# Query latents' squares behind their copy, a later first turn group, and an up projection in runs of one width

## The chip, the cores and the metric

The kernel runs on one core of one Trainium2 chip. The metric is the device time of one execution in microseconds; the time before is the median of three runs. The core has TensorE (matmuls, writing to PSUM), VectorE, ScalarE, GpSimd and SyncE, which work side by side, each through its own queue in order, and wait for each other by semaphores. The profile calls them PE, DVE, ACT, POOL and SP.

## The reference

A decoder trunk of two layers on 256 tokens of width 2048, in float32. Layer 0 mixes with stick-breaking and forgetting attention, layer 1 with latent attention; behind each mixer stands an MLP with squared ReLU. What the change touches is the latent attention and the MLPs' first matrix:

```python
def mla_mixer(h, positions, w_down, q_a_g, kv_a_g, w_uq, w_ukv, q_g, k_g, w_o):
    down = h @ w_down                                    # 2048 -> 512 + 512 + 64
    c_q, c_kv, k_pe = jnp.split(down, [512, 1024], axis=-1)
    c_q, c_kv = rmsnorm(c_q, q_a_g), rmsnorm(c_kv, kv_a_g)
    q = to_heads(c_q @ w_uq, 16)                         # 16 heads of 128 + 64
    kv = to_heads(c_kv @ w_ukv, 16)                      # 16 heads of 128 keys + 128 values
    ...
    q, k = rmsnorm(q, q_g), rmsnorm(k, k_g)              # then rotary positions on the 64
    return causal_softmax_attention(q, k, v) @ w_o

def squared_relu_mlp(h, w_up, w_down):                   # 2048 -> 8192 -> 2048
    return jnp.square(jax.nn.relu(h @ w_up)) @ w_down
```

## The kernel before

**Products in two halves.** Every float32 operand is split into a rounded half (hi) and a residual (lo), and a product is hi·hi + hi·lo + lo·hi. Weights arrive by DMA in loads of four k-tiles; half a load is a *piece*. For each piece ScalarE writes hi (`split_hi`, L766) and VectorE lo (`split_lo`, L1075), four pieces ahead of TensorE (`AHEAD`); the next hi into a buffer waits until TensorE has used the old piece (`pieces_used`).

**The order of the work.** `plan_steps` writes out by hand, for each piece `n` of a mixer, the steps that follow it. TensorE, ScalarE and VectorE walk the same list: TensorE runs the piece and then its part of the steps; the other two run their parts of the same steps in the list's order, the split of piece `n + 4` among them (normally first). An engine that waits in a step holds everything behind it in its queue.

**Layer 1's mixer.** Its chunks come in the order ckva, ckvb (key latents, 512, and the shared rotary key), cq (query latents), then ukv0, uq0, ukv1, uq1 up to uq7: for each *group* g of two heads the keys and values (`ukv{g}`, 512 wide, two pieces of twelve matmuls) and the queries (`uq{g}`, 384 wide, two pieces). Around them stand these steps:
- `rows` of a chunk: ScalarE copies the sums out of PSUM (L833); for ukv and uq it first squares them with a sum (`square_rows`, L838). Two pairs of banks serve in turn, so a chunk may not start before the rows of the chunk two before it are read (`rows_read`).
- `latent_scale(which)`: the root of a latent's mean square. ScalarE squares the latents in SBUF (`nat`), VectorE takes the mean (L1082), ScalarE a logarithm and an exponential (`power`, L774 and L775), VectorE corrects them; uq0's rows wait for the result (`scale_ready`).
- `turn_c(n)`: transposes of latents, two tiles of TensorE, a scaled copy by ScalarE (L933), a residual by VectorE (L1273). ukv0 needs 0 and 1, uq0 needs 2 and 3 (`c_ready`).
- `turn(t)`, t = 16 + 3g + 0, 1, 2: transposes of a group's scaled keys, scaled queries and rotary parts (L1670) into the one bank TURN, which VectorE then copies out (L1263, L1258, L1261). A turn waits until the turn before it is copied out (`turn_read`). The keys and queries are scaled by VectorE behind the rows of uq (L1228, L1231), the rotary parts by GpSimd.
- ScalarE's rows of `uq{g}` wait for `turned` to reach 16 + 3g: all turns of the group before are done, since the same buffers are written. VectorE's part of these rows waits for ScalarE's squares.
- `scores`, `probs`, `out` of the heads of group g, from the second piece of ukv{g+2} on.

In the plan before, latent_scale(1) follows piece 1 of uq0, and turns 16, 17 and 18 follow the second piece of ukv1 and the two pieces of uq1; every later group has the same places. The list of the first two groups' turn steps is sorted so that VectorE copies the turn ahead of the split.

**The up projection** of an MLP block (`piece_cols`, eight pieces for each of four column chunks, four blocks in each layer) takes the weights as the stationary operand. For each of a piece's two k-tiles and two groups of two column tiles it runs two matmuls of one kind and then two of the other: hi weights against both halves of the activations (512 columns, L1590), lo weights against the hi half (256 columns, L1593). The order of the two kinds is fixed but for the first k-tile.

Of the kernel before, what the change touches and what calls it, by code (L numbers as in the profile page):

```python
# [31 lines left out]
P = 128  # L32
T = 256
# [3 lines left out]
HD = 128  # L37
# [12 lines left out]
N = 512  # L50
AHEAD = 4
SLOTS = 4
COL_GROUPS = ((0, 1), (2, 3))


GROUPS = 4
# [169 lines left out]
def plan_steps():  # L226
# [47 lines left out]
    at(AT1["ckva"] + 5, ("norm_rows", 0))  # L274
    at(AT1["cq"] + 1, ("turn_c", 0))
    at(AT1["cq"] + 2, ("turn_c", 1))
    at(AT1["cq"] + 4, ("latent_scale", 0))
    at(AT1["ukv0"], ("turn_c", 2), ("turn_c", 3))
    at(AT1["uq0"], ("latent_scale", 1))
    for g in range(8):  # L280

        b = [AT1[f"ukv{g + i}"] if g + i < 8 else AT1["o0"] for i in range(2)]
        k, q, ropes = (16 + 3 * g + i for i in range(3))
        if g < 7:
            at(b[1] + 1, ("turn", k))
            at(b[1] + 2, ("turn", q))
            at(b[1] + 3, ("turn", ropes))
    for g in range(6):
        b = [AT1[f"ukv{g + i}"] if g + i < 8 else AT1["o0"] + 4 * (g + i - 8) for i in range(4)]
        h = 16 + 2 * g  # L290
# [13 lines left out]
    for at_, chunks in ((AT0, MIX0), (AT1, MIX1)):  # L304
        for name, kind, loads in chunks:
            if name == "q0":
                pass
            elif kind == "rows":
                at(at_[name] + 2 * len(loads) - 1, ("rows", name))

    at(AT1["o0"] - 1, ("squares", "uq7"))
    for n in (AT0["o0"] - 1, AT0["o0"] + 5, AT1["o0"] - 1, AT1["o0"] + 5):
# [21 lines left out]
def build(nc, x, positions, ln_mix_g, ln_mlp_g, sf_w_in, sf_b_f, fox_q_g, fox_k_g, sf_w_o,  # L334
# [4 lines left out]
    with ExitStack() as ctx:  # L339
# [404 lines left out]
        def _(act):  # L744
# [106 lines left out]
                elif name[:2] == "uq" and name != "uq7":  # L851
                    power(8)

            def latent_scale(which):

                act.wait_ge(rows_read, ROWS1[("ckvb", "ukv0")[which]] + 1)
                square_rows([(nat[:, which, tt], mix[:, 7168 + tt * N:7168 + (tt + 1) * N], st[:, 0, tt:tt + 1], None)
                             for tt in range(TT)])
                power(TT)

            def late_squares(no):

# [5 lines left out]
            def wide_rows(name, last_piece, no):  # L868
# [3 lines left out]
                if name[:3] == "ukv":  # L872
                    if name == "ukv0":
                        act.wait_ge(scale_ready, 1)
                    junk = mix[:, 7168:8192].rearrange("p (s n) -> p s n", s=TT) if name == "ukv0" else nat[:, 1]
                    square_rows([(banks[tt][:, 2 * e * HD:2 * e * HD + NOPE], junk[:, tt, e * NOPE:(e + 1) * NOPE],
                                  st[:, 0, 4 + 2 * tt + e:5 + 2 * tt + e], s_c[:, 0, tt:tt + 1])
                                 for tt in range(TT) for e in range(2)])
                elif name[:2] == "uq":
                    if name == "uq0":  # L880
                        act.wait_ge(scale_ready, 2)
                    else:
                        act.wait_ge(turned, 16 + 3 * int(name[2]))
                    if name != "uq7":
                        square_rows([(banks[tt][:, e * QKD:(e + 1) * QKD], sq_tok[:, 2 * tt + e],
                                      st[:, 0, 2 * tt + e:1 + 2 * tt + e], s_c[:, 1, tt:tt + 1])
                                     for tt in range(TT) for e in range(2)])
                elif name in ("q2", "k2", "q3", "k3"):
                    square_rows([(banks[tt][:, e * HD:(e + 1) * HD], mix[:, 6144 + (4 * tt + e) * HD:6144 + (4 * tt + e + 1) * HD],
                                  st[:, 0, 4 * tt + e:4 * tt + e + 1], r_tok[:, tt:tt + 1]) for tt in range(TT) for e in range(4)])  # L890
# [84 lines left out]
            def mixer(chunks, start, rows_no, norm):  # L975
                n = start
                for name, kind, loads in chunks:
                    for j in range(2 * len(loads)):
                        for what, arg in steps_after(n):
# [10 lines left out]
                                rows(arg, n, rows_no[arg])  # L990
                            elif what == "squares":
                                late_squares(rows_no[arg])
                            elif what == "latent_scale":
                                latent_scale(arg)
                            elif what == "first_r":
                                power(TT)
                            elif what == "square_x":
# [63 lines left out]
        def _(dve):  # L1061
# [170 lines left out]
                     .then_inc(q_scaled, 1)  # L1232

            def latent_scale(which):
                dve.wait_ge(squared, 5 + 2 * which)
                power(TT, 1.0 / RANK)
                v.tensor_tensor(s_c[:, which], st[:, 3, 0:TT], st[:, 2, 0:TT], ALU.mult).then_inc(scale_ready, 1)
                if which == 0:
# [79 lines left out]
            def mixer(chunks, start, rows_no, norm):  # L1318
                n = start
                for name, kind, loads in chunks:  # L1320
                    for j in range(2 * len(loads)):
# [12 lines left out]
                        for what, arg in steps:  # L1334
# [30 lines left out]
                            elif what == "turn":  # L1365
                                if arg >= 16:
                                    turn(arg)
                            elif what not in ("square_x", "squares"):
                                {"turn_c": turn_c, "probs": probs, "out": head_out}[what](arg)
                        n += 1  # L1370

# [156 lines left out]
        def _(pe):  # L1528
# [50 lines left out]

            def piece_cols(n, j, set_, src):  # L1580

                for i in range(2):
                    k = 2 * j + i
                    for group in COL_GROUPS:
                        for which in ((0, 1) if k == 0 else (1, 0)):
                            for m in group:
                                bank = psum[:, 4 * set_ + m]
                                cols = slice(i * N + m * P, i * N + (m + 1) * P)
                                if which == 0:
                                    last = mm(bank, half_piece(n, 0)[:, cols], src[:, k].rearrange("p s t -> p (s t)"),  # L1590
                                              start=(k == 0), stop=(k == KT - 1))
                                else:
                                    last = mm(bank[:, T:2 * T], half_piece(n, 1)[:, cols], src[:, k, 0],  # L1593
                                              start=False, stop=False)
                return last


# [345 lines left out]
```

## Time and profile before

| What | Value |
|---|---|
| Median of three runs | 2060.84 us (2060.48 to 2061.94) |
| The profiled execution | 2061.12 us, of which its span 2059.4 us |
| TensorE busy | 2049.9 us, 10488 matmuls |
| VectorE, ScalarE, GpSimd busy | 1454.0, 1109.2, 216.6 us |
| Up projection, 512 wide (L1590) | 2048 matmuls, 639.0 us busy |
| Up projection, 256 wide (L1593) | 2048 matmuls, 398.0 us busy |
| DMA | 432.35 MB, 210 GB/s |

Times inside the profile count from the start of the span. Matmuls overlap: a 512-wide one is recorded with 0.39 us, but the next starts some 0.23 us after it, so TensorE's speed is read from the distance between starts and not from busy time. In a timeline the brackets give the engine's idle time ahead of the row and what ended it.

### The profile page before, as it was taken

What the parts mean: (1) busy time and instruction counts of PE and PEld (TensorE: products, weight loads), DVE (VectorE), ACT (ScalarE), POOL (GpSimd) and SP (SyncE); (2) the same over time, 40 slices, a digit from 0 to 9 for tenths busy, and PEclk for the clock granted to TensorE, in tenths of its full rate; (3) what the DMA queues carried; (4) which work ended last, traced back from release to release, by engine and by line L of the source; (5) the groups of instructions that cost most, each with busy time, mean ns of one, the idle gap of its engine ahead of it and who ended that gap; (6) DMA issues with size and microseconds to landing.
All of it is one profiled execution on the core that took longest, in us unless ns stands there. A gap on an engine that the chain in (4) does not pass through costs nothing.

```text
span 2059.4 us, 26460 instructions
## 1 busy us (share of the span) xinstructions
PE 2049.9 (100%) x10488; PEld 1749.7 (85%) x10488; DVE 1454.0 (71%) x1967; ACT 1109.2 (54%) x1592; POOL 216.6 (11%) x317
## 2 busy tenths in 40 slices
PE   9999999999999999999999999999999999999999
PEld 7898888888888888888889888888888888888887
DVE  6556556566866877786696688557786696687777
ACT  6555565454644544554466686444554464454454
POOL 0000000020210120110010255001110021012010
PEclk9999999999999999999999999999999999999999
DMA  8555555585885795696576433568696588679565
GB/s 283 175 154 182 170 164 163 184 253 197 256 268 191 234 290 179 198 307 202 191 240 190 149 124 123 170 205 244 197 304 206 192 262 263 201 226 289 180 198 191
DMA packets 222195, 432.35 MB, mean 210 GB/s; under 512 B 12076, under 2 KB 26488, under 8 KB 222072
## 3 DMA queue, kind: packets, MB, share of 16 engines
q1 hardware_dynamic: 200520, 380.29, 55.4%
q0 software_dynamic: 21504, 50.34, 10.7%
q8 instruction: 84, 1.38, 0.3%
q14 instruction: 39, 0.32, 0.0%
q10 hardware_dynamic: 48, 0.02, 0.0%
HBM read 428.52 MB, written 2.10 MB: 209 GB/s over the span
## 4 chain that ended last, share of the span: by engine, by line
PE 98%; ACT 1%; DVE 1%; DMA 0%; issue 0%; SPq 0%; DVEq 0%; ACTq 0%
PE psum L1590 23%; PE psum L1542 14%; PE psum L1544 14%; PE psum L1543 14%; PE psum L1593 12%; PE psum L1824 5%; PE psum L1825 5%; PE psum L1826 5%; PE psum L1670 1%; PE psum L1757 1%; PE psum L1614 1%; PE psum L1734 0%; PE psum L1758 0%; DMA raw<-in_sf_w_in 0%; PE psum L1714 0%; PE psum L1715 0%
## 5 line engine op out<-in xcount | busy, mean ns | idle before, releaser
L1075 DVE TENSOR_TENSOR halves<-raw,halves 128x1024 fp32r<-128x1024 f32 (+2 forms) x736 | 853.1, 1166 | 445.0 <-ACT halves L766 441.1
L766 ACT CAST halves<-raw 128x1024 fp32r<-128x1024 f32 (+2 forms) x736 | 727.8, 1000 | 598.8 <-PE psum L1544 301.7
L1590 PE MATMUL psum<-h,halves 128*128 128x512 f32 x2048 | 639.0, 395 | 0.0
L1593 PEld LDWEIGHTS psum<-h,halves 128*128 128x128 f32 x2048 | 380.1, 188 | 87.7
L1593 PE MATMUL psum<-h,halves 128*128 128x256 f32 x2048 | 398.0, 278 | 0.0
L1542 PE MATMUL psum<-halves,a 128*128 128x512 f32 x828 | 325.3, 393 | 0.0
L1544 PE MATMUL psum<-halves,a 128*128 128x512 f32 x828 | 322.6, 390 | 0.0
L1543 PE MATMUL psum<-halves,a 128*128 128x512 f32 x828 | 322.3, 389 | 0.0
L1590 PEld LDWEIGHTS psum<-h,halves 128*128 128x128 f32 x2048 | 314.3, 189 | 2.8
L1542 PE MATMUL psum<-halves,h 128*128 128x512 f32 (+4 forms) x572 | 213.4, 373 | 0.2 <-DVE h L1146 0.2
L1544 PE MATMUL psum<-halves,h 128*128 128x512 f32 (+4 forms) x572 | 206.9, 362 | 0.0
L1543 PE MATMUL psum<-halves,h 128*128 128x512 f32 (+4 forms) x572 | 206.5, 361 | 0.0
L1544 PEld LDWEIGHTS psum<-halves,a 128*128 128x128 f32 x828 | 155.4, 188 | 32.8
L1543 PEld LDWEIGHTS psum<-halves,a 128*128 128x128 f32 x828 | 155.6, 188 | 31.5
L1542 PEld LDWEIGHTS psum<-halves,a 128*128 128x128 f32 x828 | 155.5, 188 | 31.3
L679 POOL DMA_DIRECT2D mix<-in_mlp_w_down x48 | 29.9, 641 | 1192.7 <-DVE halves L1075 1118.0
L1544 PEld LDWEIGHTS psum<-halves,h 128*128 128x128 f32 x572 | 107.5, 188 | 15.5
L1542 PEld LDWEIGHTS psum<-halves,h 128*128 128x128 f32 x572 | 107.7, 188 | 14.2 <-issue 0.4
L1543 PEld LDWEIGHTS psum<-halves,h 128*128 128x128 f32 x572 | 107.8, 188 | 13.9
L1824 PE MATMUL psum<-halves,a 128*128 128x512 f32 x272 | 105.8, 389 | 0.0
L1825 PE MATMUL psum<-halves,a 128*128 128x512 f32 x272 | 105.8, 389 | 0.0
L1826 PE MATMUL psum<-halves,a 128*128 128x512 f32 x272 | 105.8, 389 | 0.0
(267 smaller groups left out, 2082.2 us busy)
## 6 DMA issues: line engine op xcount, KB each, us to landing
raw<-in_mlp_w_up SPq DMA_DIRECT2D x128, 1024.0 KB, 6.1
raw<-in_mlp_w_down SPq DMA_DIRECT2D x128, 1024.0 KB, 5.2
mix<-in_mlp_w_down POOLq DMA_DIRECT2D x192, 256.0 KB, 7.1
raw<-in_sf_w_in SPq DMA_DIRECT2D x41, 1024.0 KB, 5.1
raw<-in_sf_w_o SPq DMA_DIRECT2D x16, 1024.0 KB, 5.1
raw<-in_mla_w_o SPq DMA_DIRECT2D x16, 1024.0 KB, 5.1
raw<-in_mla_w_ukv SPq DMA_DIRECT2D x8, 1024.0 KB, 5.4
raw<-in_sf_w_in SPq DMA_DIRECT2D x14, 512.0 KB, 3.9
```

Of the source, the lines that this page charges most:

```text
L679: pool.dma_start(u[:, 0], b11).then_inc(u_loaded[m % 2], 16)
L766: nc.scalar.copy(half_piece(n, 0), raw_piece(n)).then_inc(hi_done, 1)
L1075: v.tensor_tensor(half_piece(n, 1), raw_piece(n), half_piece(n, 0).bitcast(F32), ALU.subtract)\
L1542: mm(bank, x_hi, hi[:, i], start=(k == 0), stop=False)
L1543: mm(bank, x_hi, lo[:, i], start=False, stop=False)
L1544: last = mm(bank, x_lo, hi[:, i], start=False, stop=(k == total_kts - 1))
L1590: last = mm(bank, half_piece(n, 0)[:, cols], src[:, k].rearrange("p s t -> p (s t)"), start=(k == 0), stop=(k == KT - 1))
L1593: last = mm(bank[:, T:2 * T], half_piece(n, 1)[:, cols], src[:, k, 0], start=False, stop=False)
L1614: ins = nc.tensor.transpose(psum[:, bank + i // 2, col:col + P], x_tok[:, tt, k * P:(k + 1) * P], ident[:])
L1824: mm(bank, x_hi, w_hi, start=start, stop=False)
L1825: mm(bank, x_hi, w_lo, start=False, stop=False)
L1826: return mm(bank, x_lo, w_hi, start=False, stop=stop)
```

## The change

Three edits:
- The query latents' squares become a step of their own, `latent_squares`, for both latents. Those of the query latents follow the last piece of cq, behind the copy of its rows, into the same junk space. latent_scale(1), now the root alone, moves from piece 1 of uq0 to piece 1 of ukv0, behind turn_c(2) and turn_c(3). VectorE's count for it goes from 7 to 6. ukv0's own squares write their unused results to `nat`, as the other groups' do.
- For group 0 alone, turns 16, 17 and 18 follow the two pieces of uq1 and the first piece of ukv2, each one piece later.
- `piece_cols` runs all eight matmuls of one width and then all eight of the other; which comes first alternates from piece to piece, so that runs of 16 of one width form across pieces. The number of matmuls and their operands are the same.

```diff
--- before.py
+++ after.py
@@ -50,7 +50,6 @@
 N = 512
 AHEAD = 4
 SLOTS = 4
-COL_GROUPS = ((0, 1), (2, 3))
 
 
 GROUPS = 4
@@ -274,17 +273,17 @@
     at(AT1["ckva"] + 5, ("norm_rows", 0))
     at(AT1["cq"] + 1, ("turn_c", 0))
     at(AT1["cq"] + 2, ("turn_c", 1))
-    at(AT1["cq"] + 4, ("latent_scale", 0))
-    at(AT1["ukv0"], ("turn_c", 2), ("turn_c", 3))
-    at(AT1["uq0"], ("latent_scale", 1))
+    at(AT1["cq"] + 4, ("latent_squares", 0), ("latent_scale", 0))
+    at(AT1["ukv0"], ("turn_c", 2), ("turn_c", 3), ("latent_scale", 1))
     for g in range(8):
 
         b = [AT1[f"ukv{g + i}"] if g + i < 8 else AT1["o0"] for i in range(2)]
         k, q, ropes = (16 + 3 * g + i for i in range(3))
         if g < 7:
-            at(b[1] + 1, ("turn", k))
-            at(b[1] + 2, ("turn", q))
-            at(b[1] + 3, ("turn", ropes))
+            late = int(g == 0)
+            at(b[1] + 1 + late, ("turn", k))
+            at(b[1] + 2 + late, ("turn", q))
+            at(b[1] + 3 + late, ("turn", ropes))
     for g in range(6):
         b = [AT1[f"ukv{g + i}"] if g + i < 8 else AT1["o0"] + 4 * (g + i - 8) for i in range(4)]
         h = 16 + 2 * g
@@ -307,6 +306,7 @@
                 pass
             elif kind == "rows":
                 at(at_[name] + 2 * len(loads) - 1, ("rows", name))
+    at(AT1["ukv0"] - 1, ("latent_squares", 1))
 
     at(AT1["o0"] - 1, ("squares", "uq7"))
     for n in (AT0["o0"] - 1, AT0["o0"] + 5, AT1["o0"] - 1, AT1["o0"] + 5):
@@ -851,12 +851,11 @@
                 elif name[:2] == "uq" and name != "uq7":
                     power(8)
 
-            def latent_scale(which):
-
-                act.wait_ge(rows_read, ROWS1[("ckvb", "ukv0")[which]] + 1)
+            def latent_squares(which):
+
+                act.wait_ge(rows_read, ROWS1[("ckvb", "cq")[which]] + 1)
                 square_rows([(nat[:, which, tt], mix[:, 7168 + tt * N:7168 + (tt + 1) * N], st[:, 0, tt:tt + 1], None)
                              for tt in range(TT)])
-                power(TT)
 
             def late_squares(no):
 
@@ -872,8 +871,7 @@
                 if name[:3] == "ukv":
                     if name == "ukv0":
                         act.wait_ge(scale_ready, 1)
-                    junk = mix[:, 7168:8192].rearrange("p (s n) -> p s n", s=TT) if name == "ukv0" else nat[:, 1]
-                    square_rows([(banks[tt][:, 2 * e * HD:2 * e * HD + NOPE], junk[:, tt, e * NOPE:(e + 1) * NOPE],
+                    square_rows([(banks[tt][:, 2 * e * HD:2 * e * HD + NOPE], nat[:, 1, tt, e * NOPE:(e + 1) * NOPE],
                                   st[:, 0, 4 + 2 * tt + e:5 + 2 * tt + e], s_c[:, 0, tt:tt + 1])
                                  for tt in range(TT) for e in range(2)])
                 elif name[:2] == "uq":
@@ -990,8 +988,10 @@
                                 rows(arg, n, rows_no[arg])
                             elif what == "squares":
                                 late_squares(rows_no[arg])
+                            elif what == "latent_squares":
+                                latent_squares(arg)
                             elif what == "latent_scale":
-                                latent_scale(arg)
+                                power(TT)
                             elif what == "first_r":
                                 power(TT)
                             elif what == "square_x":
@@ -1232,7 +1232,7 @@
                      .then_inc(q_scaled, 1)
 
             def latent_scale(which):
-                dve.wait_ge(squared, 5 + 2 * which)
+                dve.wait_ge(squared, 5 + which)
                 power(TT, 1.0 / RANK)
                 v.tensor_tensor(s_c[:, which], st[:, 3, 0:TT], st[:, 2, 0:TT], ALU.mult).then_inc(scale_ready, 1)
                 if which == 0:
@@ -1365,7 +1365,7 @@
                             elif what == "turn":
                                 if arg >= 16:
                                     turn(arg)
-                            elif what not in ("square_x", "squares"):
+                            elif what not in ("square_x", "squares", "latent_squares"):
                                 {"turn_c": turn_c, "probs": probs, "out": head_out}[what](arg)
                         n += 1
 
@@ -1579,19 +1579,18 @@
 
             def piece_cols(n, j, set_, src):
 
-                for i in range(2):
-                    k = 2 * j + i
-                    for group in COL_GROUPS:
-                        for which in ((0, 1) if k == 0 else (1, 0)):
-                            for m in group:
-                                bank = psum[:, 4 * set_ + m]
-                                cols = slice(i * N + m * P, i * N + (m + 1) * P)
-                                if which == 0:
-                                    last = mm(bank, half_piece(n, 0)[:, cols], src[:, k].rearrange("p s t -> p (s t)"),
-                                              start=(k == 0), stop=(k == KT - 1))
-                                else:
-                                    last = mm(bank[:, T:2 * T], half_piece(n, 1)[:, cols], src[:, k, 0],
-                                              start=False, stop=False)
+                for which in ((0, 1) if j % 2 == 0 else (1, 0)):
+                    for i in range(2):
+                        k = 2 * j + i
+                        for m in range(4):
+                            bank = psum[:, 4 * set_ + m]
+                            cols = slice(i * N + m * P, i * N + (m + 1) * P)
+                            if which == 0:
+                                last = mm(bank, half_piece(n, 0)[:, cols], src[:, k].rearrange("p s t -> p (s t)"),
+                                          start=(k == 0), stop=(k == KT - 1))
+                            else:
+                                last = mm(bank[:, T:2 * T], half_piece(n, 1)[:, cols], src[:, k, 0],
+                                          start=False, stop=False)
                 return last
```

## Rows read from the trace of the kernel before

**Rows 1.** The page, part 4: the ended-last chain's shares of the span by engine.

```profile
PE 98%; ACT 1%; DVE 1%; DMA 0%; issue 0%; SPq 0%; DVEq 0%; ACTq 0%
```

**Rows 2.** Timeline of TensorE, first latent heads: start us, us, work, [idle <- releaser].

```profile
1155.99 0.39 PE L1542 MATMUL psum<-halves,a 128*128 128x512 f32 x1
...
1164.36 0.66 PE L1670 MATMUL psum<-ident,mix 128*128 128x128 f32 x4 [2.72 <-DVE mix L1228]
...
1167.51 0.63 PE L1670 MATMUL psum<-ident,mix 128*128 128x128 f32 x4 [0.42 <-DVE mix L1263]
...
1170.07 0.60 PE L1670 MATMUL psum<-ident,mix 128*128 128x128 f32 x4
...
1173.27 0.39 PE L1542 MATMUL psum<-halves,a 128*128 128x512 f32 x1
...
1176.14 0.66 PE L1670 MATMUL psum<-ident,mix 128*128 128x128 f32 x4
```

**Rows 3.** Timeline of ScalarE in the same stretch, from the query latents on.

```profile
1138.49 0.63 ACT L838 ACTIVATE mix<-nat 128x512 f32<-128x512 f32 x1
...
1140.06 0.20 ACT L774 ACTIVATE st<-st 128x2 f32<-128x2 f32 x1 [0.24 <-DVE st L1082]
...
1146.39 1.26 ACT L833 ACTIVATE nat<-psum,r_tok 128x512 f32<-128x512 f32 x2
...
1148.42 1.05 ACT L766 CAST halves<-raw 128x1024 fp32r<-128x1024 f32 x1 [0.77 <-PE psum L1544]
...
1152.01 1.05 ACT L766 CAST halves<-raw 128x1024 fp32r<-128x1024 f32 x1 [1.07 <-PE psum L1544]
...
1154.34 1.28 ACT L833 ACTIVATE mix<-psum,s_c 128x512 f32<-128x512 f32 x2
...
1159.22 0.42 ACT L838 ACTIVATE nat<-psum,s_c 128x192 f32<-128x192 f32 x1 [0.25 <-DVE s_c L1237]
...
1171.01 0.41 ACT L838 ACTIVATE nat<-psum,s_c 128x192 f32<-128x192 f32 x1
```

**Rows 4.** Timeline of VectorE in the same stretch.

```profile
1149.50 1.22 DVE L1075 TENSOR_TENSOR halves<-raw,halves 128x1024 fp32r<-128x1024 f32 x1 [2.02 <-ACT halves L766]
...
1150.64 1.65 DVE L1273 SCALAR_TENSOR_TENSOR h<-psum,gains,h 128x256 fp32r<-128x256 f32 x4
...
1164.95 1.76 DVE L1075 TENSOR_TENSOR halves<-raw,halves 128x1024 fp32r<-128x1024 f32 x1
...
1166.63 0.74 DVE L1263 TENSOR_SCALAR mix<-psum,gains 128x512 f32<-128x512 f32 x1
...
1172.35 0.85 DVE L1261 COPY tables<-psum 64x256 f32<-64x256 f32 x2
...
1176.74 1.75 DVE L1075 TENSOR_TENSOR halves<-raw,halves 128x1024 fp32r<-128x1024 f32 x1
```

**Rows 5.** Windows, TensorE alone: stretch, us, busy us (x matmuls), granted clock, DMA share, GB/s.

```profile
577.08:666.28 89.20, 89.20 (x513) 1.00 0.68 212
494.80:577.07 82.27, 82.27 (x364) 1.00 0.80 252
129.17:130.60 1.43, 1.43 (x13) 1.00 0.00 0
155.73:157.12 1.39, 1.39 (x8) 1.00 0.54 72
493.64:494.79 1.15, 1.15 (x7) 1.00 1.05 411
```

**Rows 6.** Windows of TensorE where it ran nothing, and of its first work.

```profile
1161.90:1164.30 2.40, 0.00 (x0) 1.00 0.82 303
2055.80:2057.80 2.00, 0.00 (x0) 1.00 0.53 205
2057.90:2059.30 1.40, 0.00 (x0) 0.50 0.14 54
1.58:6.44 4.86, 4.86 (x21) 1.00 0.83 247
```

## The prediction, made before the changed kernel ran

> **What bounds the kernel now.** I read the chain that ended last first: TensorE is 98% of it [rows 1], so an edit matters by what it does to the distance between matmul starts, or by a wait of TensorE that it removes or makes. Next I read TensorE's timeline where the first two edits are. The waits in brackets stand at the first group of heads only: 2.72 us before the transposes of turn 16 and 0.42 before turn 17, both for VectorE [rows 2]. Turn 19, the next group's first, came at 1176.14 where its piece, begun at 1173.27, ends after some 2.72 us (twelve matmuls of 0.227), at 1175.99: 0.15 us of wait [rows 2]. Then ScalarE and VectorE in the same stretch, to see what was late [rows 3, 4]. uq0's rows start on ScalarE at 1159.22 and waited for the query latents' scale, which is computed just ahead of them [rows 3]; turn 16 needs the keys that are scaled behind those rows. At most 3.3 us of waits are to be won. Last I read the up projection, where the third edit is, in windows [rows 5], and the granted clock [rows 6].
>
> **Edit 1: the squares early, the root behind the turned copies.** I follow ScalarE in the times of before.
> The latents' copy ends at 1146.39 + 1.26 = 1147.65. Two squares took from 1138.49 to the start of the wait ahead of 1140.06, which is 1139.82, so 1.33 us [rows 3]. The next weight split, at 1148.42 before, starts at 1148.9, half a microsecond later: it waited for TensorE, so most of the squares lie in idle time. The turned copies behind it and VectorE's residuals (1150.64, 1.65 us) move by the same 0.5, so the residuals end at 1152.8 [rows 3, 4].
> The root is now queued behind them, and ScalarE waits in it for VectorE's mean. From VectorE's start to ScalarE's next work it is about 0.6 us (0.24 of wait, two activations of 0.20, a little overlap [rows 3]), so the next split starts at 1153.4, not 1152.01: 1.36 late. Queued behind are ukv0's rows, whose copies ended at 1154.34 + 1.28 = 1155.62 and now end at 1157.0. Who waits: ukv1 writes the banks that ukv0's rows are read from, so TensorE starts ukv1 at 1157.04 instead of 1155.99, a new stall of 1.05 us [rows 2, 3]. The later residuals delay uq0 by some 0.2, within that.
> What is removed: at uq0 the squares (1.33), the root (0.6) and the wait of 0.25 for it are gone from ScalarE's queue ahead of uq0's rows. These start at 1159.22 + 1.36 - 1.33 - 0.6 - 0.25 = 1158.4, 0.8 earlier [rows 3]. The keys are ready at 1163.5 instead of 1164.3. Alone, edit 1 would be worth about 0.8 us.
>
> **Edit 2: the first group's turns a piece later.** TensorE goes from 1157.04 through two pieces of 2.75 and 2.72 and one of 2.11 to 1164.63, and turn 16 finds its keys ready: the 2.72 us are gone. Turn and piece take 0.41 + 2.17 (1167.51 to 1170.07, 2.56 [rows 2]), so turn 17 comes at 1167.2. It needs turn 16 copied out of the one shared bank. VectorE, free at 1164.95 - 0.82 = 1164.13, now has two residual splits ahead of that copy (1.68 from start to start with GpSimd at work, the second 1.6, as GpSimd stops meanwhile), then the copy of 0.74: 1168.15 [rows 4]. Turn 17 goes at 1168.2, a stall of 1.0. A turn and a 512-wide piece take 3.20 (1170.07 to 1173.27 [rows 2]), so turn 18 goes at 1171.4, against 1170.07 before. TensorE has not even gained here.
>
> What is queued behind turn 18 decides. ScalarE may not start uq1's rows before turn 18 is done (the `turned` wait: they overwrite what it reads). Before, turn 18 stood behind the same piece as those rows; now it is one piece behind them, and the wait holds ScalarE's queue, and VectorE's, which waits for the squares. ScalarE's rows started at 1171.01, and start now 0.65 after turn 18, at 1172.05: 1.04 later [rows 2, 3]. The second group's scaled keys and queries, and the residual split behind them (1176.74 before [rows 4]), come 1.04 later too, at 1177.8. On VectorE turn 18's copies out of the bank now stand behind all of that: the split spends 1.7, the three copies 1.2 (two took 0.85), to 1180.65 [rows 4]. Turn 19 may not overwrite the bank earlier, and goes at 1180.7 instead of 1176.14. Meanwhile TensorE has one piece to do, to 1174.5, and then stands still for 6 us. **Edits 1 and 2 together: 4.5 us slower.** If VectorE's splits took 1.22 as at 1149.50, where GpSimd is idle, and not 1.75 [rows 4], turn 17 would hardly wait and turn 19 would go at 1179.2: 3.0. That is the lower end, 4.7 with a tenth more at each hand-over the upper; I keep 4.5, since the longer duration is the one of this stretch. Downstream everything shifts alike.
>
> **The clock.** During the 2.4 us in which TensorE ran nothing at 1161.9 the granted clock stayed 1.00; after its last matmul it was still 1.00 for 2.0 us and then 0.50, the lower of the levels [rows 6]. A still stand of 6 us is longer than either, so I expect the clock at 0.50 when turn 19 resumes. How long it stays there no row in the middle shows. At the start of the program 21 transposes took 4.86 us, 0.23 each against 0.11 to 0.13 later [rows 2, 6] (the clock column is not yet filled there), so work at half rate for up to 4.9 us, half of which is lost: 0 to 2.4 us. I take 1.6, as a stall three times as long as one that did nothing speaks for a fall, and part of the 4.9 may pass otherwise.
> The Trainium skill, "TensorE: Matmul & The Clock Gate", section "Why this matters for your kernels", advises against idle gaps between bursts of matmuls because the clock falls back. That speaks against edit 2; by it the sum holds the 1.6, without it the change gives 2064.7. The end of this trace agrees, the shorter gap at 1161.9 shows that not every gap does it.
>
> **Edit 3: runs of one width.** A block's up projection runs 512 matmuls, half of them 512 and half 256 wide, two by two, in 89.20 us (x513 counts one that was still running): 5.575 us for 32 [rows 5]. The change makes runs of 16. In a stream of 512 the step is 82.27 / 363 = 0.2267; a stretch of twelve 256-wide ones right behind 512-wide ones took 1.43, 0.1195 each, so a narrow run costs nothing at its start [rows 5]. 16 of each are 5.539, and 0.036 per 32, times 4096 / 32 = 128, is 4.6 us: the most to win. But the first wide matmuls behind narrow ones are slow: six steps behind a 264-wide run took 1.39 to 1.40 instead of 1.360, and five behind the last 256-wide pair of a block 1.15 to 1.16 instead of 1.134 [rows 5]. That is 0.02 to 0.04 once per 32, against a gain of 0.036. What is left is +0.5 to -2 us. I take -0.6, nearest to the long narrow run. Splits and evictions wait for the ends of pieces, which stay; no wait is added.
>
> **The sum.** The profiled execution took 2061.12 us, span 2059.4 and 1.7 around it; the median of the runs is 2060.84, 0.3 lower. 4.5 + 1.6 - 0.6 = +5.5: 2066.6 against the profiled execution, 2066.3 against the median, which I forecast. With the bounds (3.0 to 4.7, 0 to 2.4, -2 to 0.5) it goes from 2061.8 to 2068.4.
>
> **The rivals.**
> 1. The clock holds through the stall: 2060.84 + 4.5 - 0.6 = 2064.7. For it: the gap at 1161.9. Against it: the end of the program.
> 2. The runs pay in full, the other side: not slower. If the slow first steps belong to whatever else changed at those places and the run settles at once, edit 3 is worth -4.6 and the sum is 2060.84 + 4.5 + 1.6 - 4.6 = 2062.3, within 0.2%. Its place is the first six wide matmuls behind sixteen narrow ones, its price 0.03 us 128 times, and it decides from a step there of under 0.228. Both stretches that show the passage speak against it.
> 3. The stall goes and none comes back: faster. If uq1's keys were ready when ukv2's second piece ends at 1174.5, TensorE would win 3.3 and the 0.6: 2056.9. It decides at ScalarE's start of uq1's rows, which would have to be at 1169.4 or earlier and can't be before turn 18 at 1171.4. Against it is the order of the waits itself; for it, only that I placed one wrongly.
> 4. Both passages between widths cost 0.036: (0.072 - 0.036) x 128 = +4.6 instead of -0.6, 2071.5. The stretch at 129.17 speaks against it.
>
> **How the numbers follow.** The forecast 0.57, rival 1 0.18, rival 2 0.12, rival 3 0.08, rival 4 0.05. A measurement of this kernel tells about 0.2%, 4.1 us, from no change, so the bound is 2065.0. Slower: nine tenths of the forecast, 0.4 of rival 1, all of rival 4: 0.64. Faster: rival 3: 0.08. Same: the rest, 0.28. The range goes from 2062.0, which takes in most of rival 2, to 2068.4, the upper end of the forecast, and leaves out rivals 3 and 4 and a little of rival 2.
>
> **What would show it.** In the profile after: TensorE's wait before turn 16 gone, one of about 1 us at ukv1 for ukv0's copies, 1.0 before turn 17, and one of about 6 us before turn 19 whose releaser is VectorE's copy of turn 18 (edits 1 and 2); a clock of 0.50 behind it; an up projection of 89.1 us a block against 89.20, with steps of 0.12 in the narrow runs and 0.23 to 0.24 at the head of the wide ones (edit 3). It is wrong if turn 19 finds the bank free, if the clock never leaves 1.00, or if a block's up projection falls below 88.8.

## The result, and the profile after

| | Before | After |
|---|---|---|
| Median of 12 runs each | 2061.18 us (2060.48 to 2061.94) | 2066.15 us (2065.08 to 2066.99) |
| Ratio after / before | | 1.0023 (1.0015 to 1.0031) |
| The profiled execution, its span | 2061.12 us, 2059.4 us | 2066.03 us, 2064.3 us |

The changed kernel is 5.0 us slower. The forecast was 2066.3 us, a loss. Parts 1 and 4 of the page of after show nothing of it: TensorE is busy 1 us longer in a span that is 4.9 longer, and the chain is TensorE's still [rows 1].

```profile
span 2064.3 us, 26460 instructions
...
PE 2050.9 (99%) x10488; PEld 1758.4 (85%) x10488; DVE 1455.0 (70%) x1967; ACT 1109.4 (54%) x1592; POOL 217.2 (11%) x317
...
PE 97%; ACT 1%; DVE 1%; DMA 0%; issue 0%; SPq 0%; DVEq 0%; ACTq 0%
```

The timelines show it. To compare two kernels I count each one's times from the start of the query latents' copy on ScalarE, the last work that no edit of layer 1 has touched: 1146.39 before [rows 3], 1145.40 after. Of these 0.99 us, some 0.6 come from edit 3 in the four MLP blocks of layer 0 (0.14 each, below); the rest is scatter, since four kernels here whose up projection is that of before have this copy anywhere between 1145.92 and 1146.39.

TensorE of after, first latent heads (start us, us, work, [idle <- releaser]), to be read against [rows 2]:

```profile
1151.16 0.41 PE L1542 MATMUL psum<-halves,h 128*128 128x384 f32 x1 [0.18 <-DVE h L1273]
...
1155.90 0.50 PE L1542 MATMUL psum<-halves,a 128*128 128x512 f32 x1 [0.33 <-ACT mix L833]
...
1163.58 0.60 PE L1669 MATMUL psum<-ident,mix 128*128 128x128 f32 x4
...
1167.07 0.63 PE L1669 MATMUL psum<-ident,mix 128*128 128x128 f32 x4 [0.80 <-DVE mix L1263]
...
1170.29 0.60 PE L1669 MATMUL psum<-ident,mix 128*128 128x128 f32 x4
...
1179.70 1.09 PE L1669 MATMUL psum<-ident,mix 128*128 128x128 f32 x4 [6.04 <-DVE tables L1261]
```

The rows of L1669 are turns 16, 17, 18 and 19. The 2.72 us before turn 16 are gone; 0.80 before turn 17 and 6.04 before turn 19 have come. The brackets understate the short waits: at 1155.90 TensorE is 0.9 late against [rows 2], and the bracket has 0.33.

ScalarE in the same stretch, against [rows 3]: the copy that is the zero of the times, the root with its wait for VectorE's mean, the start of uq0's rows, and uq1's rows, which waited 3.87 us until TensorE had done turn 18.

```profile
1145.40 1.26 ACT L833 ACTIVATE nat<-psum,r_tok 128x512 f32<-128x512 f32 x2
...
1151.91 0.20 ACT L774 ACTIVATE st<-st 128x2 f32<-128x2 f32 x1 [1.48 <-DVE st L1082]
...
1157.17 0.45 ACT L838 ACTIVATE nat<-psum,s_c 128x192 f32<-128x192 f32 x1
...
1171.01 0.42 ACT L838 ACTIVATE nat<-psum,s_c 128x192 f32<-128x192 f32 x1 [3.87 <-PE psum L1669]
```

VectorE, against [rows 4]: two residual splits ahead of turn 16's copy (L1263), then, for the next group, the scaled keys and queries, one split, and only then the copies of turn 18 out of the one bank.

```profile
1162.95 3.31 DVE L1075 TENSOR_TENSOR halves<-raw,halves 128x1024 fp32r<-128x1024 f32 x2
1166.18 0.74 DVE L1263 TENSOR_SCALAR mix<-psum,gains 128x512 f32<-128x512 f32 x1
...
1175.30 0.77 DVE L1228 TENSOR_TENSOR mix<-mix,st 128x512 f32<-128x512 f32 x1
1175.99 0.80 DVE L1231 TENSOR_TENSOR mix<-mix,st 128x512 f32<-128x512 f32 x1
1176.71 1.74 DVE L1075 TENSOR_TENSOR halves<-raw,halves 128x1024 fp32r<-128x1024 f32 x1
1178.38 0.41 DVE L1258 COPY mix<-psum 128x256 f32<-128x256 f32 x1
1178.71 0.84 DVE L1261 COPY tables<-psum 64x256 f32<-64x256 f32 x2
```

Windows of TensorE (stretch, us, busy us (x matmuls), granted clock, DMA share, GB/s): first the stall and what follows, against [rows 6], then a block's up projection, a narrow run, the five first wide steps behind it and the eleven others, against [rows 5].

```profile
1173.70:1177.40 3.70, 0.00 (x0) 1.00 0.03 13
1177.50:1179.60 2.10, 0.00 (x0) 0.50 0.00 0
1179.70:1184.28 4.58, 4.58 (x16) 0.50 0.01 4
1184.30:1189.00 4.70, 4.70 (x31) 1.00 0.50 149
...
576.55:665.61 89.06, 89.06 (x513) 1.00 0.68 213
589.50:591.41 1.91, 1.91 (x17) 1.00 1.08 297
591.41:592.57 1.16, 1.16 (x7) 1.00 1.04 401
592.57:595.06 2.49, 2.49 (x12) 1.00 1.06 405
```

The clock fell to the lower of its two levels (0.50 is 1.2 GHz) inside the stall, and TensorE then worked 4.58 us at half rate, so half of that, 2.3 us, is lost.

### The profile page after: what moved, and what is told of

It reads as the page before. It is cut to its first block, busy times and chain, and to the rows that moved or that the text cites. A ratio compares the mean times of both kernels' runs of the same rounds, so it can differ in the third digit from the quotient of the medians.

```text
span 2064.3 us, 26460 instructions
## 1 busy us (share of the span) xinstructions
PE 2050.9 (99%) x10488; PEld 1758.4 (85%) x10488; DVE 1455.0 (70%) x1967; ACT 1109.4 (54%) x1592; POOL 217.2 (11%) x317
## 4 chain that ended last, share of the span: by engine, by line
PE 97%; ACT 1%; DVE 1%; DMA 0%; issue 0%; SPq 0%; DVEq 0%; ACTq 0%
PE psum L1589 23%; PE psum L1542 14%; PE psum L1544 14%; PE psum L1543 14%; PE psum L1592 12%; PE psum L1823 5%; PE psum L1824 5%; PE psum L1825 5%; PE psum L1669 1%; PE psum L1756 1%; PE psum L1613 1%; ACT nat L838 0%; PE psum L1733 0%; DVE halves L1075 0%; PE psum L1757 0%; PE psum L1713 0%
## 5 line engine op out<-in xcount | busy, mean ns | idle before, releaser
L1589 PE MATMUL psum<-h,halves 128*128 128x512 f32 x2048 | 489.8, 391 | 0.0
L1589 PEld LDWEIGHTS psum<-h,halves 128*128 128x128 f32 x2048 | 376.3, 188 | 72.9
L1592 PEld LDWEIGHTS psum<-h,halves 128*128 128x128 f32 x2048 | 262.6, 191 | 10.0
L1592 PE MATMUL psum<-h,halves 128*128 128x256 f32 x2048 | 266.1, 283 | 0.0
```

## The experiments

The theory: turn 18, one piece later, holds uq1's rows on ScalarE; VectorE's copies of turn 18 are queued behind what those rows feed; so turn 19 stalls for 6 us, which lets the clock fall and costs twice. Edit 1 gains about a microsecond and edit 3 less. Rivals: that the loss belongs to the late turns as a whole or to the root's new wait; that the clock has no part in it; that edit 3 saves nothing or much more.

This table has what the profiles say of all kernels (us; "from copy" is the distance from the latents' copy; in brackets the idle time that the row shows):

| Kernel | Turn 16 from copy | Turn 19 from copy | Median, with that of before beside it |
|---|---|---|---|
| before | 17.97 [2.72] | 29.75 | |
| after | 18.18 | 34.30 [6.04] | 2066.15, 2061.18 |
| a1, edit 1 alone | 16.93 [0.71] | 28.72 | 2059.89, 2061.67 |
| a2, edit 2 alone | 17.99 | 35.32 [6.05] | 2067.93, 2061.67 |
| a3, edit 3 alone | 17.96 [2.70] | 30.65 | 2060.38, 2061.67 |
| a4, edits 1 and 3 | 16.95 [0.74] | 28.74 | 2058.60, 2061.67 |
| b1, after, kept busy | 18.16 | 34.31 [0.84] | 2063.82, 2061.56 |
| b2, after, turn 18 back | 18.18 | 29.97 | 2059.87, 2061.56 |
| b3, after, turn 18 copied first | 18.18 | 30.70 [2.45] | 2060.73, 2061.56 |
| c1, runs of eight | 17.97 [2.71] | 29.76 | 2062.36, 2061.56 |
| d1, root at uq0 | 17.61 [1.96] | 30.35 | 2059.92, 2061.30 |
| d2, root at once | 16.79 [0.45] | 28.59 | 2058.27, 2061.58 |
| d3, before, kept busy | 17.97 [0.53] | 29.77 | 2060.78, 2061.58 |

### One edit at a time

Each edit of the diff above, alone on the kernel before, and the first and third together (the diff without its lines with `late`).

> Edit 1 alone (squares behind their copy, root behind the turned copies), turns and up projection as before. My sum: the wait before turn 16 shrinks from 2.72 us to about 0.8, a new one of about 1 us comes at ukv1 for ukv0's copies, net 0.8 us faster than before (2061.2): 2060.4. Rival, the root's wait in ScalarE's queue costs what the removed squares give: 2061.2, or slower.

Measured: 2059.89 us (2059.65 to 2060.22), ratio 0.9991 (0.9982 to 1.0000).

> Edit 2 alone (first group's turns a piece later). My sum: turn 16 still waits some 0.8 us for its keys, turn 17 about 2 us for the bank, turn 18 goes at about 1172.2 and turn 19 some 9.4 us behind it, at 1181.6 instead of 1176.14: 5.5 us slower, and 2.1 more because the clock falls in the stall, as in the changed kernel's profile. Together +7.6: 2068.8. Rival, edit 2 is harmless by itself and the stall comes from the two edits together: 2061 to 2062.

Measured: 2067.93 us (2067.51 to 2069.68, five executions), ratio 1.0032 (1.0019 to 1.0044).

> Edit 3 alone (runs of one width). By the changed kernel's profile a block's up projection takes 89.07 us instead of 89.21, so 1.1 us less in all eight: 2060.1, no change in any wait. Rival, runs paid in full: 4.6 us less, 2056.6. Rival, runs cost something: above 2061.5.

Measured: 2060.38 us (2059.36 to 2060.83), ratio 0.9993 (0.9985 to 1.0002).

> The changed kernel without edit 2: turns where they were. If edit 2 holds the whole loss, edits 1 and 3 are left: 0.8 + 1.1 faster than before, 2059.3, no wait of TensorE over 3 us and the clock at 1.00 throughout the mixer. Rival, edit 1's early squares bring part of the loss: 2062 or above.

Measured: 2058.60 us (2058.33 to 2058.90), ratio 0.9985 (0.9976 to 0.9994).

TensorE in a1, turn 16:

```profile
1163.09 0.66 PE L1670 MATMUL psum<-ident,mix 128*128 128x128 f32 x4 [0.71 <-DVE mix L1228]
```

TensorE in a4, turn 19, without a wait:

```profile
1174.23 0.66 PE L1668 MATMUL psum<-ident,mix 128*128 128x128 f32 x4
```

TensorE in a2, turns 17, 18 and 19:

```profile
1168.62 0.63 PE L1671 MATMUL psum<-ident,mix 128*128 128x128 f32 x4 [1.97 <-DVE mix L1264]
...
1171.84 0.60 PE L1671 MATMUL psum<-ident,mix 128*128 128x128 f32 x4
...
1181.24 1.08 PE L1671 MATMUL psum<-ident,mix 128*128 128x128 f32 x4 [6.05 <-DVE tables L1262]
```

The windows of a2 from the fall of the clock to turn 19, and from there to its rise:

```profile
1178.06:1181.20 3.14, 0.00 (x0) 0.50 0.00 0
1181.24:1184.87 3.63, 3.63 (x13) 0.50 0.02 5
```

The loss is edit 2's: alone it has the whole stall, and without it there is none. By the table the edits add up at turn 19. Edit 1 brings it 1.03 earlier on the kernel before (29.75 to 28.72) and 1.02 earlier beside edit 2 (35.32 to 34.30); edit 2 brings it 5.57 later (29.75 to 35.32) and 5.56 beside the others (28.74 to 34.30). Edit 3 brings nothing there, but a block's up projection takes 89.07 us from its first matmul to the first behind it, instead of 89.21: over eight blocks 1.1 us. So the root's new wait is no part of the loss. Edits 1 and 3 together beat both kernels.

In medians edit 1 alone is worth 1.78, not 1.03, and a3's turn 19 comes 0.9 later than before's though nothing is changed there. Both go back to the clock. The windows of a3 show the stretch of the stall before turn 16, turn 16 and what follows it, and the work behind that.

```profile
1160.50:1162.90 2.40, 0.00 (x0) 1.00 0.82 307
1163.10:1166.40 3.30, 3.21 (x12) 0.50 0.00 0
1166.50:1170.00 3.50, 3.50 (x24) 1.00 0.34 64
```

Here the clock fell at the end of the 2.7 us before turn 16. In the profiled execution of before it did not [rows 6]. Which one is the rule is settled by d3, below. The 3.3 us at half rate would cost 1.6 us, and only 0.9 arrive at turn 19: turn 17's wait of 0.42 us [rows 2] is gone in a3, so part of the loss falls into it.

Two of the expected sums were off, in part for the same reason. Against the before beside it a2 is 6.3 us slower, where I had 7.6: the stall before turn 16 is gone, and with it the 0.8 us that the clock costs there in before (d3, below); and from turn 19 on a2 works 3.63 us at half rate, after 4.58. And a4 is 3.1 us faster, where I had 1.9: to the 1.0 of edit 1 and the 1.1 of edit 3 comes the same 0.8.

### The stall before turn 19

b1 is the kernel after with 48 transposes more, whose results nothing reads, ahead of turn 19's waits, so that TensorE works through the stall:

```diff
+                    if t == 19:
+                        for _ in range(48):
+                            nc.tensor.transpose(PROBS[:, 0:P], ident[:], ident[:])
```

> The changed kernel with 48 transposes of a constant (results unused) on TensorE ahead of turn 19's waits, 5.3 us of work that ends before turn 19 may go. If the low clock behind the stall costs 2 us, the clock stays at 1.00 and the time falls from 2066.15 to about 2064.1, with turn 19 where it was. Rival, the clock costs nothing here and the stall is all: 2066.1, or more if the transposes reach into turn 19.

Measured: 2063.82 us (2063.57 to 2065.09), ratio 1.0012 (1.0003 to 1.0021). TensorE in the stall and at turn 19, and the window behind it:

```profile
1173.70 5.40 PE L1662 MATMUL psum<-ident 128*128 128x128 f32 x48
...
1179.94 0.63 PE L1672 MATMUL psum<-ident,mix 128*128 128x128 f32 x4 [0.84 <-DVE tables L1261]
```

```profile
1179.90:1184.00 4.10, 4.06 (x26) 1.00 0.00 0
```

Turn 19 comes at the same place (34.31 from the copy), the clock is 1.00 behind it, and 2.33 us are back (2066.15 to 2063.82). The traces give nearly the same without the medians: turn 20 follows turn 19 after 3.87 us here and after 6.08 in after, 2.2 less. So the clock's share of the loss is 2.2 to 2.3 us, and the rest is the stall itself. The Trainium skill ("TensorE: Matmul & The Clock Gate", section "Why this matters for your kernels") advises against idle gaps between bursts of matmuls, since the clock falls back; this pair of kernels agrees and puts the price at 2.3 us here.

b2 puts turn 18 alone back to its old step:

```diff
-            at(b[1] + 3 + late, ("turn", ropes))
+            at(b[1] + 3, ("turn", ropes))
```

> The changed kernel with turn 18 alone put back, behind the same piece as uq1's rows; turns 16 and 17 stay late. If the one place of turn 18 makes the stall: uq1's rows start at about 1170 on ScalarE, a wait of some 2 us comes before turn 18 for the bank, none over 1 us before turn 19, which goes at about 1175.3 instead of 1179.7; the clock stays at 1.00. Together 6 us less than the changed kernel: 2060. Rival, late turns cost as such: 2064 to 2066.

Measured: 2059.87 us (2059.61 to 2061.16), ratio 0.9992 (0.9984 to 1.0001). TensorE, turns 17, 18 and 19:

```profile
1167.08 0.63 PE L1669 MATMUL psum<-ident,mix 128*128 128x128 f32 x4 [0.78 <-DVE mix L1263]
...
1169.48 0.63 PE L1669 MATMUL psum<-ident,mix 128*128 128x128 f32 x4 [1.77 <-DVE mix L1263]
...
1175.40 0.61 PE L1669 MATMUL psum<-ident,mix 128*128 128x128 f32 x4
```

Turn 18 now waits 1.77 us for turn 17's copy, and still turn 19 comes 4.3 us earlier than in after, without a wait. It is turn 18's place alone, not that of the other two, that makes the stall.

b3 leaves turn 18 late on TensorE, but VectorE copies it out before its part of uq1's rows instead of behind the split:

```diff
+                                if arg == "uq1":
+                                    turn(18)
                                 rows(arg, rows_no[arg])
...
-                                if arg >= 16:
+                                if arg >= 16 and arg != 18:
                                     turn(arg)
```

> The changed kernel, but VectorE copies turn 18 out of the bank ahead of its part of uq1's rows and not behind them; TensorE's and ScalarE's order is unchanged. That separates the two halves of the stall before turn 19. By my sum turn 19 then waits for its keys alone, goes at 1176.1 instead of 1179.7, a stall of 2.7 instead of 6.3 us, and the clock stays at 1.00: 5.6 us less than the changed kernel, 2060.5. Rival, the hold of uq1's rows is the whole stall and the bank adds nothing: 2066.

Measured: 2060.73 us (2059.94 to 2062.29), ratio 0.9996 (0.9987 to 1.0005). TensorE at turn 19, and VectorE's first copy of turn 18:

```profile
1171.33 0.42 DVE L1258 COPY mix<-psum 128x256 f32<-128x256 f32 x1 [1.60 <-PE psum L1671]
...
1176.52 0.66 PE L1671 MATMUL psum<-ident,mix 128*128 128x128 f32 x4 [2.45 <-DVE mix L1228]
```

The copy runs 7.5 us earlier (25.51 from the latents' copy, 32.98 in after); turn 19 waits 2.45 us and for another thing, the keys of L1228. So of the 6.04 us 3.6 (34.30 - 30.70) were the copy in a queue that was itself held, and the rest are the keys, late because ScalarE was held for turn 18.

### The runs of one width

c1 has edit 3 alone, without the alternation: the order of the widths is the same in all of a chunk's eight pieces but the last, so the runs are mostly of eight.

```diff
-                for which in ((0, 1) if j % 2 == 0 else (1, 0)):
+                for which in ((0, 1) if j < 7 else (1, 0)):
```

> Edit 3 alone, but without the alternation (wide first in all pieces but the last of a chunk): runs of 8, seven instead of four passages from narrow to wide in each of 32 chunks. If a passage costs 0.02 us net, as the steps in the changed kernel's profile sum up to, 96 more of them cost 1.9 us against runs of 16: 2062.0. Rival, passages cost nothing and the gain of runs has another source: as runs of 16, 2060.1.

Measured: 2062.36 us (2060.99 to 2062.88), ratio 1.0003 (0.9994 to 1.0012). A block takes 89.31 us against 89.07 with runs of sixteen:

```profile
576.65:665.96 89.31, 89.31 (x514) 1.00 0.69 214
```

Over eight blocks that is 1.9 us. A chunk of eight pieces passes from wide to narrow and back seven times here and four times in the change, so three more for each of 32 chunks, 96 in all: 20 ns for each passage there and back.

The steps in the trace of after give the same. Averaged by their place in the run, the first five wide steps behind a narrow run take 233.3, 235.9, 228.3, 232.5 and 230.8 ns and all later ones 226.7, so the passage costs 27 ns; the first two narrow ones behind a wide run take 113.3 and 119.2 and all later ones 120.0, so the way back gives 7.5. Together 20. That is the reason why a longer run gains, and why it can't gain much: 32 matmuls in two runs of sixteen are 20 ns above the two steady rates, where before they were 29.

### Where the root should stand, and what the kernel before loses to the clock

d1 is a4 with only the squares early, and the root where it was, at uq0. A wait comes with it: ukv0's rows write to `nat`, which the squares read, and may not start before those are done. ScalarE shows no idle time there.

```diff
-    at(AT1["ukv0"], ("turn_c", 2), ("turn_c", 3), ("latent_scale", 1))
+    at(AT1["ukv0"], ("turn_c", 2), ("turn_c", 3))
+    at(AT1["uq0"], ("latent_scale", 1))
...
+                        act.wait_ge(squared, 6)
```

> A version for use: edit 3, and of edit 1 only the early squares; the root stays at uq0, and the turns where they were. ScalarE then does not wait for VectorE ahead of ukv0's rows, so ukv1 starts without a stall, and uq0's rows start 1.3 us earlier than before. With 1.1 us from the runs: 2.4 us faster than before, 2058.8, the wait before turn 16 at 1.4 instead of 2.72 us. Rival, the root's place makes no difference: 2059.3 as with both parts of edit 1.

Measured: 2059.92 us (2058.61 to 2060.73), ratio 0.9993 (0.9984 to 1.0002): a miss, 1.1 us above what I expected. VectorE's split and mean, ScalarE at the root, TensorE at turn 16 and the window behind it:

```profile
1155.46 0.96 DVE L1076 TENSOR_TENSOR halves<-raw,halves 128x768 fp32r<-128x768 f32 x1 [2.06 <-ACT halves L766]
1156.34 0.16 DVE L1083 TENSOR_SCALAR st<-st 128x2 f32<-128x2 f32 x1
...
1156.53 0.20 ACT L774 ACTIVATE st<-st 128x2 f32<-128x2 f32 x1 [1.10 <-DVE st L1083]
...
1163.08 0.70 PE L1670 MATMUL psum<-ident,mix 128*128 128x128 f32 x4 [1.96 <-DVE mix L1229]
```

```profile
1163.60:1166.90 3.30, 3.30 (x13) 0.50 0.00 0
```

I had taken the root's wait to be gone with the squares early. At uq0 VectorE's mean is queued behind VectorE's own split, and ScalarE waits 1.10 us for it; turn 16's wait is 1.2 us longer than in a4, and the clock falls again. The root's wait behind the turned copies (1.48 us in after) is the smaller harm.

d2 is a4 with the root right behind the squares:

```diff
-    at(AT1["ukv0"], ("turn_c", 2), ("turn_c", 3), ("latent_scale", 1))
+    at(AT1["ukv0"], ("turn_c", 2), ("turn_c", 3))
...
-    at(AT1["ukv0"] - 1, ("latent_squares", 1))
+    at(AT1["ukv0"] - 1, ("latent_squares", 1), ("latent_scale", 1))
```

> Edits 1 and 3, turns where they were, but the root right behind the squares, ahead of the split and the turned copies. VectorE is idle there, so ScalarE should wait some 0.2 us for it, not 1.5 as behind the turned copies. The copies come 0.75 us later (uq0 starts about 1.1 us late instead of 0.34), ukv0's and uq0's rows 1.1 earlier, and the keys are ready about when TensorE comes to turn 16: 1 us less than with edit 1's place (2058.6), 2057.6. Rival, the later start of uq0 is carried on to turn 16 and eats it: 2058.6.

Measured: 2058.27 us (2057.74 to 2058.96), ratio 0.9984 (0.9976 to 0.9993). ScalarE at the root and at the split ahead of uq0's rows, TensorE at turn 16:

```profile
1148.19 0.20 ACT L773 ACTIVATE st<-st 128x2 f32<-128x2 f32 x1 [0.23 <-DVE st L1081]
...
1156.22 0.84 ACT L765 CAST halves<-raw 128x768 fp32r<-128x768 f32 x1 [0.94 <-PE psum L1543]
...
1162.11 0.66 PE L1668 MATMUL psum<-ident,mix 128*128 128x128 f32 x4 [0.45 <-DVE mix L1227]
```

The root's wait is 0.23 us there, but of the microsecond that I expected at turn 16 only 0.16 came (16.95 to 16.79): ScalarE is early at uq0, and the split ahead of uq0's rows now waits 0.94 us for TensorE. It is the fastest kernel of the study; against a4 its 0.3 us are not told apart by the intervals.

d3 is the kernel before with 20 transposes, their results unread, ahead of turn 16's wait, as in b1 but with `t == 16`.

> The kernel before with 20 transposes of a constant (results unused) on TensorE ahead of turn 16's wait, 2.2 us of work inside the 2.7 us stall. If the clock falls in that stall in those executions whose mean clock is recorded as 0.999, all executions should now show 1.000, spread less, and have the median of those of before at 1.000: 2060.8. Rival, the two groups of executions have another cause: both stay, and the median stays at 2061.5.

Measured: 2060.78 us (2060.48 to 2061.09), ratio 0.9996 (0.9987 to 1.0005). TensorE and the window behind turn 16:

```profile
1161.05 2.34 PE L1663 MATMUL psum<-ident 128*128 128x128 f32 x20
...
1163.92 0.66 PE L1673 MATMUL psum<-ident,mix 128*128 128x128 f32 x4 [0.53 <-DVE mix L1228]
```

```profile
1163.90:1168.00 4.10, 3.66 (x23) 1.00 0.00 0
```

Turn 16 stands where it stood before (17.97 from the copy). In all 11 executions of d3 the mean clock was 1.000. Of the 21 executions of before beside it, 16 had 0.999 and a median of 2061.76 us, and 5 had 1.000 and 2060.97. d3 sits with the five. Beside the other kernels above, 56 of 75 executions of before had 0.999, and in each of the three groups their median lies 0.7 to 1.0 us above that of the rest. So the kernel before loses some 0.8 us to the clock in about three quarters of its executions, in the stall before turn 16, and the one that was profiled was of the other quarter. The fall itself is seen in the profiles of a3 and d1; for before it follows from the mean clocks and from d3. Every kernel with that stall nearly gone (a1, a4, d2) shows 1.000 in all its executions.

## Why the prediction was right, point by point

| Term | Predicted | In the traces |
|---|---|---|
| Edits 1 and 2, at turn 19 | +4.5 | +4.55 (29.75 to 34.30) |
| Clock behind the stall | +1.6 | +2.3 (b1; +2.2 from turn 19 to turn 20) |
| Edit 3 | -0.6 | -1.1 (eight blocks at 0.14) |
| Turn 22, later on | 0 | -0.2 (a short wait before it is gone) |
| Clock in before's own stall | 0 | -0.4 (below) |
| Sum | +5.5 | +5.15; the medians give +4.97 |

The 12 executions of before that the result is set against fall into two groups of six, 2060.48 to 2060.91 and 2061.46 to 2061.94 us; their mean clocks are not on record. Their median, 2061.18, is 0.4 above the median of the faster six, and that is the last term. The profiled executions can be summed without it: 4.55 + 2.2 - 1.1 - 0.2 is 5.4, their spans differ by 4.9, and of the 0.5 between 0.4 lie ahead of the latents' copy, in the scatter named above.

**Edit 1.** With after's times moved by 0.99: ukv1 was forecast for 1157.04 and came at 1156.89, uq0's rows for 1158.4 and came at 1158.16, turn 16 for 1164.63 and came at 1164.57, its stall gone. Nothing was mis-placed; the stage gains 1.03 at turn 16 where I had 0.8, 0.16 of it because ScalarE is back from the root by 1153.24 and not 1153.4. That edit 1 also keeps the clock up, I did not see.

**Edit 2.** Turn 17 was forecast for 1168.2 and came at 1168.06, turn 18 for 1171.4 and at 1171.28, uq1's rows on ScalarE for 1172.05 and at 1172.00, turn 19 for 1180.7 and at 1180.69. The chain was the one described, down to the releaser (VectorE's copy of turn 18, L1261). What carried it was to follow the `turned` wait to everything queued behind it, on ScalarE and then on VectorE; b2 and b3 confirm each of the two hand-overs.

**The clock.** The lower level came, as forecast, but 1.6 was 0.7 too little. I had shrunk the 2.4 us that the program's start gave, half of 4.86 [rows 6], because a part of it might be something else; the half-rate work in after took 4.58 us. That the start gave nearly the right size is partly luck: in a2, behind the same stall, it took 3.63 us, and behind the shorter ones of a3 and d1 3.3. Rival 1, the clock that holds, is refuted by the window of after at 0.50 and by b1.

**The clock in the 2.4 us before turn 16.** This is the step that was wrong, though the sum hid it. The row was read rightly, 1.00 in that execution, but I took one execution for a rule. In most executions of before the clock falls there and some 0.8 us go; so the reference already carried a loss that the changed kernel doesn't have at that place, and the profiled execution is the wrong one to set a median against. It also made rival 1 look better than it was.

**Edit 3.** The mechanism was right: the loss is at the head of the wide runs, not in the narrow ones. The size was off. I took 0.1195 as the narrow rate, from twelve steps right behind wide ones (1.43 / 12 is 0.1192, so even that was rounded up); the steady rate is 0.120, and the first two steps are faster, so the most to win was 29 ns per 32 matmuls and not 36. The passage there and back costs 20 ns, not 20 to 40. With that 29 - 20 = 9 ns are won per 32 matmuls, 128 times, 1.1 us. Rival 2 (the run settles at once, -4.6) needed a first step under 0.228 and it is 0.233; rival 4 (both passages cost) falls because the way back gives 7.5 ns.

**Rivals.** Rival 3, the stall that goes with none in its place, would have needed uq1's rows at 1169.4; they came at 1172.00. b2 shows what it takes: turn 18 left where it was.

The errors ran against each other: 0.7 too little for the clock, against 0.5 too little gain by edit 3, 0.2 at turn 22 and the 0.4 that before loses. The reference moved too: its median was 2060.84 us in the three executions that the forecast starts from and 2061.18 in the twelve beside the result, so a loss of 5.0 instead of 5.5 still ends 0.15 us from the forecast. The close median is in part this luck; the two placed stalls are not.

## What to carry to other kernels

When a step is moved later, look for every engine that waits on it by count and not by data, and then for what stands in those engines' queues: a transposition that was on nobody's path held ScalarE for 3.9 us and, through VectorE, TensorE for 6.0. Price a stall of TensorE with what the clock takes behind it, and look at the spread of the executions and their mean clocks before one profile is read as the rule. A wait that is shortened, not moved, is worth more than its length where the clock used to fall in it (1.78 instead of 1.03 us for edit 1).

## What the hardware showed that was not expected

- By the mean clocks, the stall of 2.7 us before turn 16 lowered the granted clock in 16 of 21 executions of one kernel and not in the other 5; 0.7 us of it (a1, a4) did so in none of 11 each. The length alone does not decide: a mean clock of 0.999 stands in 8 of 11 executions of d1 (1.96 us before turn 16), in 4 of 11 of b3 (2.45 us before turn 19) and in 3 of 11 of b2 (1.77 us before turn 18); where it fell in those of b2 and b3, no profile shows. With 20 or 48 transposes in the stall (d3, b1) the clock stayed at 1.00. What decides between the two outcomes for one kernel stays open.
- The clock was low for 6.8 us in after (1177.45 to 1184.28) and in a2 (1178.05 to 1184.87), but it fell 2.25 us before turn 19 in one and 3.2 us before it in the other, so that TensorE worked 4.58 and 3.63 us at half rate behind the same stall. In a3 and d1 it was low for 3.4 us.
- The step of a matmul of this type depends on the width of those before it: five steps of 512 behind 256-wide ones are 27 ns late in sum, two of 256 behind 512-wide ones 7.5 ns early. Why, no run here shows.
